# A mixture-of-experts stage on one core: the down slabs are issued by GpSimd instead of the sync engine

## What is computed

```python
gates, idx = lax.top_k(aff.transpose(0, 2, 1), cap)      # cap = 2 * 256 / 16 = 32
xs = h[b_ix, idx]                                        # 32 x 1024 per expert
a = jnp.einsum('becd,edf->becf', xs, w_gate)             # 1024 x 1024 per expert
u = jnp.einsum('becd,edf->becf', xs, w_up)
y = jnp.einsum('becf,efd->becd', jax.nn.silu(a) * u, w_down)
y = y * gates[..., None].astype(y.dtype)
return jnp.zeros_like(h).at[b_ix, idx].add(y)
```

## Time and profile before

| | |
|---|---|
| time, median of 3 runs | 2267.76 us (2267.06 to 2273.89) |
| the profiled execution's own time | 2271.71 us |
| its span, first to last instruction | 2269.9 us |
| TensorE busy (matmuls) | 2040.7 us, 90% |
| DVE, ACT, GpSimd busy | 894.1, 718.2, 40.7 us |
| moved by DMA | 592.33 MB, 260 GB/s over the span |
| SP's DMA queue (q1) | 586.67 MB, 65.1% of 16 engines |
| GpSimd's DMA queue (q0) | 3.70 MB, 0.4%, 1104 packets |
| chain that ended last | 69% TensorE, 24% DMA |

### The profile page before, as it was taken

The page is one execution under the profiler, slowest core; times in us unless marked ns, Lnnn a source line. Parts: engine busy times, 40 slices in busy tenths (PEclk is TensorE's granted clock), DMA queues, the critical chain, the costliest instruction groups (busy, mean ns, idle before and its releaser), DMA issues.

```text
span 2269.9 us, 38396 instructions
## 1 busy us (share of the span) xinstructions
PE 2040.7 (90%) x17052; PEld 1394.6 (61%) x17052; DVE 894.1 (39%) x1272; ACT 718.2 (32%) x1015; POOL 40.7 (2%) x65
## 2 busy tenths in 40 slices
PE   7999987888879999987788789989999999889998
PEld 6887433333328886433333248665899886758996
DVE  6444211110116444110101138446677474466774
ACT  5444111111115453111111135313444453144443
POOL 1000000000001000000000000000000000000000
PEclk9999788887889998888888889999999999999999
DMA  8236899999996257999999994022754350227540
GB/s 322 88 142 276 364 427 429 429 428 428 428 419 224 75 186 307 415 427 429 429 427 429 429 403 169 4 105 83 243 186 158 130 202 4 85 103 224 186 177 19
DMA packets 139667, 592.33 MB, mean 261 GB/s; under 512 B 5744, under 2 KB 59200, under 8 KB 114448
## 3 DMA queue, kind: packets, MB, share of 16 engines
q1 hardware_dynamic: 138432, 586.67, 65.1%
q0 software_dynamic: 1104, 3.70, 0.4%
HBM read 589.30 MB, written 1.05 MB: 260 GB/s over the span
## 4 chain that ended last, share of the span: by engine, by line
PE 69%; DMA 24%; DVE 3%; issue 2%; ACT 1%; SPq 1%; DVEq 0%; POOLq 0%; ACTq 0%; POOL 0%
PE ps L578 36%; DMA ring<-in_w_up 23%; PE ps L1182 11%; PE ps L2191 3%; PE ps L904 2%; PE ps L2006 2%; PE ps L1205 1%; PE ps L2238 1%; PE ps L1144 1%; DMA ring<-in_w_in 1%; PE ps L1214 1%; PE ps L595 1%; PE ps L1003 1%; PE ps L1099 1%; PE ps L1079 1%
## 5 line engine op out<-in xcount | busy, mean ns | idle before, releaser
L1182 PE MATMUL ps<-ring,area 128*32 128x512 f32 x1920 | 307.8, 715 | 120.9 <-DMA ring<-in_w_up 120.9
L554 DVE TENSOR_TENSOR ring_lo<-ring,slab_hi 128x2048 fp32r<-128x2048 f32 x136 | 311.3, 2292 | 225.2 <-ACT slab_hi L549 224.9
L549 ACT ACTIVATE slab_hi<-ring 128x2048 fp32r<-128x2048 f32 x136 | 260.0, 1913 | 285.0 <-PE ps L578 265.6
L1182 PEld LDWEIGHTS ps<-ring,area 128*32 128x32 f32 x1920 | 72.7, 128 | 311.4 <-issue 159.3
L578 PE MATMUL ps<-hT_hi,slab_hi 128*128 128x256 f32 x832 | 235.1, 283 | 3.0 <-DVE hT_lo L571 1.5
L578 PE MATMUL ps<-hT_lo,slab_hi 128*128 128x256 f32 x832 | 233.9, 281 | 0.0
L578 PE MATMUL ps<-hT_hi,ring_lo 128*128 128x256 f32 x832 | 232.8, 280 | 0.0
L1771 DVE TENSOR_TENSOR area<-ps,par 128x256 f32<-128x256 f32 x32 | 13.6, 425 | 477.2 <-PE ps L1144 477.2
L1205 PE MATMUL ps<-ring,area 128*32 128x512 f32 x992 | 161.9, 811 | 30.9 <-DVE area L1791 29.8
L1421 ACT ACTIVATE area<-ps 128x512 f32<-128x512 f32 x32 | 19.1, 597 | 536.1 <-PE ps L1182 536.1
L578 PEld LDWEIGHTS ps<-hT_hi,slab_hi 128*128 128x128 f32 x832 | 156.4, 188 | 4.3 <-issue 2.2
(11 more groups left out here) (384 smaller groups left out, 3165.2 us busy)
## 6 DMA issues: line engine op xcount, KB each, us to landing
ring<-in_w_up SPq DMA_DIRECT2D x62, 2048.0 KB, 20.3
ring<-in_w_down SPq DMA_DIRECT2D x62, 2048.0 KB, 21.6
ring<-in_w_gate SPq DMA_DIRECT2D x56, 2048.0 KB, 15.2
ring<-in_w_ffn_up SPq DMA_DIRECT2D x44, 1024.0 KB, 7.7
ring<-in_w_in SPq DMA_DIRECT2D x18, 2048.0 KB, 10.2
ring<-in_w_ffn_down SPq DMA_DIRECT2D x10, 2048.0 KB, 8.0
ring<-in_xattn_w_kv SPq DMA_DIRECT2D x8, 2048.0 KB, 16.6
area<-in_w_gate SPq DMA_DIRECT2D x6, 2048.0 KB, 14.0
```

What stands on the lines that cost most here:

```text
L549: return m.nc.scalar.activation(hi, whole, ACT.Copy)
L554: return m.nc.vector.tensor_tensor(lo, whole, hi, ALU.subtract)
L1182: ins = mm(ps[32 * g:32 * g + CAP, 1, :], m.tokT[:, k, :], gate_up[i][:, k % 4, (g % 2) * BANK:(g % 2 + 1) * BANK], start=k == 0, stop=k = ...
```

## The change

From the fourth expert of a layer on (e = 3 to 15) the two down slabs are issued by GpSimd, in a loop of its own, on its own DMA queue. They have semaphores of their own, `m.down[0]` and `m.down[1]`, for which TensorE waits; the counts of `m.landed[4]` and `m.landed[5]` per layer shrink by 13 slabs. SP's loop keeps up0, up1 of expert e and gate0, gate1 of expert e+1. In the first layer GpSimd's loop stands behind everything that `gpsimd_first` did, so `late1` of the second layer is issued behind it; in the second layer it stands between the issue of `fin1` and the norm of the first block's result. Slots, sizes, the waits for free slots and TensorE's order are the same.

```diff
+DOWN_LOOP = E - 3
+LANDED1_LAYER = [n + 16 * (k - DOWN_LOOP * (s >= LAST_SLOT - 1)) for s, (n, k) in enumerate(zip(LANDED1, EXPERT_SLABS))]
...
+    m.down = [ctx.enter_context(nc.semaphore(f"down_landed{h}")) for h in range(2)]
...
+def expert_slab(m, l, name, e, n):
+
+    w = m.d[name].rearrange("l e (h p c) n -> (l e) p h c n", h=2, c=4)[bass.ds(l * E + e, 1)]
+    return w[:, :, n].rearrange("o p c n -> p (o c) n")
+
+
+def gpsimd_down(m, pool, l):
+
+    with pool.Fori(3, E) as e:
+        for s in (LAST_SLOT - 1, LAST_SLOT):
+            ring_wait(m, pool, s, l * HELD1_LAYER[s] + HELD1[s] - (s == LAST_SLOT) + e)
+            pool.dma_start(slab(m, s, 4, D), expert_slab(m, l, "w_down", e, s - LAST_SLOT + 1)).then_inc(m.down[s - LAST_SLOT + 1], 16)
...
     with sp.Fori(3, E - 1) as e:
-        into_slots(GATE_SLOTS, up_down, e, e, 3)
-        ring_wait(m, sp, LAST_SLOT, l * HELD1_LAYER[LAST_SLOT] + HELD1[LAST_SLOT] - 1 + e)
-        sp.dma_start(slab(m, LAST_SLOT, 4, D), expert("w_down", e, 1)).then_inc(m.landed[LAST_SLOT], 16)
+        into_slots(GATE_SLOTS, ("w_up",), e, e)
         into_slots(0, ("w_gate",), e + 1, e - 1)
-    into_slots(GATE_SLOTS, up_down, E - 1, E - 1, 3)
-    last_down(E - 1)
+    into_slots(GATE_SLOTS, ("w_up",), E - 1, E - 1)
...
         def slab_landed(s):
-            if s == LAST_SLOT:
+            if s >= LAST_SLOT - 1 and not (first or second or third):
+                pe.wait_ge(m.down[s - LAST_SLOT + 1], 16 * (l * DOWN_LOOP - 2) + e * 16)
+            elif s == LAST_SLOT:
...
     pool.dma_start(m.soon[:, :], m.d["soon"][l + 1]).then_inc(s("soon1_loaded"), 16)
+    if l + 1 < L:
+        gpsimd_down(m, pool, l)
...
     pool.dma_start(m.fin1, m.d["fix"][:, 2 * KD:2 * KD + D]).then_inc(m.s("fin1_loaded"), 16)
+    gpsimd_down(m, pool, L - 1)
     gpsimd_rstd(m, pool, 0, "f1", "f1_sq", 16, NT, 0)
```

More of the change, by code:

```diff
@@ L93 @@
 EXPERT_SLABS = [E - 2 if s < GATE_SLOTS else E - 1 if s == LAST_SLOT else E for s in range(SLOTS)]
-LANDED1_LAYER = [n + 16 * k for n, k in zip(LANDED1, EXPERT_SLABS)]
+DOWN_LOOP = E - 3
+LANDED1_LAYER = [n + 16 * (k - DOWN_LOOP * (s >= LAST_SLOT - 1)) for s, (n, k) in enumerate(zip(LANDED1, EXPERT_SLABS))]
 HELD1_LAYER = [n + k for n, k in zip(HELD1, EXPERT_SLABS)]
@@ L776, in expert @@
     def expert(name, e, n):
-        w = d[name].rearrange("l e (h p c) n -> (l e) p h c n", h=2, c=4)[bass.ds(l * E + e, 1)]
-        return w[:, :, n].rearrange("o p c n -> p (o c) n")
+        return expert_slab(m, l, name, e, n)
     def into_slots(first, names, e, held, parts=2):
```

## The result

| | before | changed |
|---|---|---|
| median | 2269.84 us (4 runs, 2267.06 to 2273.89) | 2307.07 us (4 runs, 2298.79 to 2311.68) |
| ratio | | 1.0154 [1.0131, 1.0177] |
| profiled execution | 2271.71 us, span 2269.9 | 2311.68 us, span 2310.0 |

A forecast was written before the change was run, and what follows sets the result against it. The prediction took DMA to bound the expert stages, 29.4 us per expert where TensorE needs 24. 15 us of phase shift less 1 for w_in gave +14, from 2267.8 to 2282 us; range 2264 to 2338.

The forecast's parts named there:

- Packets of 16 KB, 52 x 144 of them: Sign of being right: the moved down slabs go uncut on GpSimd's queue; 0 us taken, 16 us kept as bound.
- The share: GpSimd's queue beside SP's in the expert stages: 43% of the DMA rate, or half with equal turns.
- 1.35 to 1: Turns between queues, from one loaded 512 KB transfer: about 1.35 SP packets for each GpSimd packet.
- Up slabs late, down slabs early, a wait in the middle of the gate/up matmuls: Signs of being right in the expert loop: down 8 us or more early, up1 6 to 10 late, wait some 4.
- A phase shift paid at the layer's end: Last expert of each layer: late up1 costs 7.5 us, 15 for two layers; bounds 0 and 9.8 each.
- Issue cost and the moved transfer at 0: GpSimd's 52 slab issues count 0, at most 10 us; late1 behind the first layer's loop 0, at most 1.4.
- The -1 for an earlier w_in: Next layer's w_in lands sooner without the last expert's down slabs in SP's queue: -1 us, once.
- The delay does not grow: DMA is idle for 0.6 us only and the period stays at 29.4.: Expert loop followed over two experts: up1 stays 6 to 10 us late, and the loop costs nothing per expert.
- 9.2 us of cover: Work still standing in SP's queue when gate0 is issued in each expert, so DMA is never short of work.
- the rival with a small share: Down slabs get too little DMA rate and TensorE waits for them: about 2340 us, chance 0.22.
- Nothing changes: Rival: order of landing in the expert stages stays, by issue order or SP packets winning: 2268 us, chance 0.18.
- Faster: Rival: two queues keep the DMA engines fuller in the expert stages: about 2258 us, chance 0.05.

The follow-up runs named there:

- Experiment 4: Changed kernel with SP issuing gate0, up0, gate1, up1 instead of gate0, gate1, up0, up1: 2287.66 and 2292.30 us, 1.0091 and 1.0088 of the kernel before.
- Experiment 7: Against the changed kernel, only down1 is issued by GpSimd and down0 stays on SP behind up1: 2280.02 us, 1.0034 of the kernel before.
- experiments 1 and 2: Changed kernel with down slabs issued by ACT on its hardware queue: 1.0107, 1.0120; changed kernel with late1 issued ahead of GpSimd's first-layer loop: 1.0116.
- experiment 5: Changed kernel with SP's order gate0, up0, gate1, up1 and the last expert's down slabs on SP: 2276.45 and 2273.94 us, 1.0026 and 1.0015.
- the first kernel of experiment 8: Changed kernel with GpSimd also waiting until up1 of the running expert has landed before it issues down0: 2358.79 us, 1.0366 of the kernel before.

## Why the prediction was right and wrong

Right:

- *Packets of 16 KB, 52 x 144 of them*: exactly.
- *The share.* I had 43% or a half by two readings; it is a half (228 to 224), so the 1.35 to 1 read from the earlier trace rows was off. In the Trainium skill ("DMA: Bandwidth & Descriptors", section on queues, rings and completion order) the engines go round robin between queues; both this stretch and that of the 4 KB packets agree. The Trainium skill's section "Issuing engines are not separate DMA queues" on the same page would have given 2268; the runs disagree with what I took from it: in this kernel, bound by DMA, a second queue is also another order of landing.
- *Up slabs late, down slabs early, a wait in the middle of the gate/up matmuls*: seen; up1 came 9.8 us after up0 in the expert shown, and the wait was 3.92 us (some 4 forecast). The forecast had the last gate/up matmuls of a layer end 6 to 10 us later; in the first stage they end 11.6 us later (681.1 against 669.5) and in the second, counted from its first gathering, 23, with the loop's loss in both.
- *A phase shift paid at the layer's end*: right in kind, and its total only by luck. Experiment 4 leaves 12 us for two layers against 15 forecast, but as -1.5 and 14.6, and 2.3 and 10.9, not as 7.5 each; the second stage lies above the bound of 9.8. The reason is one that the hand calculation did not reach: experts alternate. Experiment 7, with one slab, has 3.3 in each.
- *Issue cost and the moved transfer at 0*: experiments 1 and 2 find nothing, and in all 26 experts TensorE waits for GpSimd's slabs five times, 3.2 us in sum.
- *The -1 for an earlier w_in*: not seen. The gap of 1.23 us in the earlier trace rows is 1.08 after.

The step that failed is this one: "The delay does not grow: DMA is idle for 0.6 us only and the period stays at 29.4." From it the prediction took that the loop costs nothing per expert, and that the rate stays at 428. I followed two experts and let the matmuls of line 1182 run as in the earlier trace rows, in one block, so that gate1's slot came free as early as before. The wait in the middle of them stood in the same prediction as a sign of being right, but its effect on gate1's slot was not carried on. In the expert shown up1 lands 9.8 us behind up0, so TensorE does the first half, waits, and does the second half late. By then the down slabs are in, and SP's queue has only gate0 left, whose last bytes move 3.9 us after up1 let the second half start (1063.9 against 1059.96). gate1 is issued after 5.45 us (1065.41) and its first bytes come 0.9 later: 5.45 + 0.9 - 3.9 = 2.4 us in which DMA stands empty. The 9.2 us of cover that the prediction counted for the earlier trace rows were down slabs; the change moved just these out of the queue's tail. This loop loss is 16 of the 30 us by which the stages grew in the profiled execution (12 and 7 in two others), where the sum had 0. Idle DMA was named in the prediction as a sign of the rival with a small share; it came without a small share.

The rival with a small share was real only at 4 KB packets. "Nothing changes" fell, since turns do not go by order of issue. "Faster" fell: no stage window of a kernel with two queues shows more than the 428 of one.

Open: how much of the loss in the loop is due to the lower clock and how much to the late up1 alone; no run held the clock. By an estimate from the rows above, 28 matmuls in 3.6 us instead of 6.1 would have brought gate1's issue 2.5 us sooner, about the whole gap of this expert. Open is also why the two losses don't add up (experiment 5). Open too is what makes the stages 10 us longer in one execution and 30 in another of the same kernel, and the 2 to 5 us of the stages that remain in experiment 5.

## What to carry to other kernels

In a kernel bound by DMA like this one, one queue in order of need is a schedule: a second queue took every other packet, however late its data was wanted, and what it prefetched was paid by what was urgent. Before moving transfers off a queue, ask what is left in it at the moment when the last late slab lands, and whether the next issue comes before that runs out; where two slots come free together, issue into both before waiting for a later one. Carry a hand calculation of a ring on, with the consumer's waits put in, until the pattern repeats, and look at which part of the pattern the last round falls on. And take two causes one at a time and together: here each edit alone won little, and both won nearly all.

## What the runs showed of the hardware

- Two queues took turns by packet: SP's and GpSimd's 228 to 224 at 16 KB and 136 to 142 at 16 KB against 4 KB, SP's and ACT's hardware queue 112 to 113. ACT's queue in GpSimd's place gave 1.0107 and 1.0120 against 1.0103 to 1.0154.
- A slab cost the same on GpSimd's queue as on SP's: with both edits of experiment 5 the stages moved 428 GB/s, as with SP alone.
- After a wait of TensorE of 6.94 us the granted clock was 0.50, and after a further one of 3.92 us 0.59: 28 matmuls took 6.09 us, against 3.63 at 1.00.
- With both queues empty, the first bytes moved 0.9 us after SP's issue (1065.41) and, in the first kernel of experiment 8, 1.2 us after GpSimd's (541.66). Where SP issued within 0.1 us of GpSimd there (508.73), GpSimd's first bytes came after 3.4 us.
